# Moving the gates' softmax, the turning of the chosen indices and the first one-hots from behind run U into its last units

## The chip, the cores and the metric

The kernel runs on one core of a Trainium2 chip, in one launch. The metric is device time in microseconds (us). A core has five engines that run their own instruction streams and meet at semaphores: PE (TensorE, matmuls; PEld are its weight loads), ACT (ScalarE), DVE (VectorE), POOL (GpSimd) and SP (SyncE, which here issues the weights' DMAs). SBUF is the on-chip memory, PSUM the memory that matmuls write to.

## The reference

Two transformer blocks on 256 tokens of width 1024, in float32. Each block ends with a PEER layer: a mixture of 16,384 tiny experts of which each token picks 16 for each of 8 heads. Cut to what matters here:

```python
s_top, i_top = lax.top_k(s, 16)                  # on both halves of a query: 128 keys each
cand = s_top[..., 0, :, None] + s_top[..., 1, None, :]
best, ci = lax.top_k(cand.reshape(..., 256), 16)
i1, i2 = i_top[0][ci // 16], i_top[1][ci % 16]
e    = i1 * 128 + i2                             # which expert
gate = softmax(best, axis=-1)
act  = gelu(einsum("thkd,td->thk", u[e], x))
out  = einsum("thk,thkd->td", gate * act, v[e])
```

## The kernel before

The kernel gathers nothing. It works through *all* experts densely, in four stages for each block (b = 1, 2):

1. **Run U** (`u1`, `u2`): 128 units. A unit is one 128x1024 piece of `u`, multiplied with all 256 tokens; GELU of the product goes to `dense` (in `big`).
2. **The gates and indices.** While U runs, DVE does the top-16 searches in pieces between its other work: 64 steps, the last after unit 115. They leave `chosen`: for each token and each of its 128 picks i1, i2 and the score, tokens on partitions. Behind U come: subtract the best score (DVE, L1531 and L1532), exp (ACT, L1097), sum, reciprocal and scale (DVE, L1535 to L1537), a copy of `iota` to PSUM (L1539), the turn of `chosen` into picks on partitions (PE, six transposes, L748) and its copy back as `chosenT` and `neg_gate` (DVE, L1542 and L1543). The semaphore `ch_t` (printed as chosen_copied) then says that the turned arrays are there.
3. **The gate map**: for every token a 128x128 matrix of gates, made as a matmul of two one-hot matrices: hot1 (a 1 at i1, scaled by the gate) and hot2 (a 1 at i2). Tokens go in 64 maps of 4 tokens, in 8 groups of 8 maps (j = 0 to 7). Each token needs one hot1 tile of 128x128. POOL makes them for 14 of a group's 32 tokens (`POOL_HOTS`: slots j = 1, 3, 5, 7; L463). DVE makes those of slots 0 and 4 four at a time (L1555) and ACT scales them (L1105). ACT makes the other 10 with Abs and Relu (L1118, L1125). DVE makes all hot2, 8 tokens at a time (L1551, helper `hots`), and multiplies each pair of finished maps into `dense` (L1563, helper `apply`). PE makes a map of 4 tokens (L766), which the profile records as 8 matmuls.
4. **Run V** (`v1`, `v2`): 128 units of `v` against `dense`.

In U and V each weight tile is split into a high and a low float32r half: ACT makes `hi` (L984), DVE makes `lo` = raw - hi (L1619 in U, L1322 elsewhere), and PE multiplies three times (L573 and L575 need `hi`, L578 needs `lo`). `hi` and `lo` have a ring of 4 slots, which is 2 units, so ACT makes unit u's halves when PE has finished unit u-2. ACT also takes each unit's product from PSUM with GELU (L1019).

Order: there is no scheduler. Each engine's stream is written out by hand. PE and ACT issue the first group of 4 units of U straight, and the other 31 in a hardware loop (`Fori`); DVE's stream for U is straight throughout. POOL's one-hots wait for `ch_t`, and from the second group on also for PE: slot j of group g overwrites slot j of group g-1, so it waits until that map has been made (`wmap`, printed as gate_map). hot2 lies in `act_hi` and `act_lo`, which U's matmuls read; so DVE waits for U's last output (`taken`, printed as outs_taken) before it makes any. hot1 lies in `scores`, which is free when the last search is done.

Of the kernel before, what the change touches and what calls it, by code (L numbers as in the profile page):

```python
# [26 lines left out]
ALU = mybir.AluOpType  # L27
# [3 lines left out]
P = 128  # L31
# [15 lines left out]
EXP_TANH = "exp_and_others"  # L47
MAPS = 8
DVE_HOTS = (0, 4)
POOL_HOTS = ((1, 4), (3, 3), (5, 4), (7, 3))  # L50
ACT_HOTS = ((2, range(4)), (3, range(3, 4)), (6, range(4)), (7, range(3, 4)))

# [109 lines left out]
def two_blocks_kernel(nc, xT_in, memT_in, cols_in, front1, front2, u1, v1, u2, v2, biasA_in, gatew_in, keys_in,  # L162
                      ada_in, c_in, out):
    with ExitStack() as ctx:
# [192 lines left out]
        def is_static(v):  # L357
            return isinstance(v, int)

        def groups(eng, r, body, peel=1):  # L360

            n = r.units // GROUP
            for g in range(min(peel, n)):
                body(g)
            if n > peel:
                with eng.Fori(peel, n) as g:
                    body(g)


# [183 lines left out]
        def _(pe):  # L553
# [82 lines left out]
                    if after is not None:  # L636
                        after(u)

            def run(name, event=None, after=None, peel=None):

                r = RUNS[name]
                if event is not None:
                    pe.wait_ge(act_ready, 2 * EV[event] + 1)
                if r.kind != "O" and r.out0 and name not in CHAINED:
                    pe.wait_ge(taken, r.out0)

                def body(g):
                    for j in range(min(GROUP, r.units)):
                        for h in range(2):
                            if r.kind == "K":  # L650
                                outs_free(r, (g * GROUP + j) * 2 + (r.out0 + h))
                            elif h == 0 and r.kind != "O":
                                outs_free(r, g * GROUP + (r.out0 + j))
                            if event is not None and h == 1 and is_static(g) and j == 0:
                                pe.wait_ge(act_ready, 2 * EV[event] + 2)
                            half(r, g, j, h)
                        if after is not None and is_static(g):
                            after(g * GROUP + j)

                if r.units < GROUP:  # L660
                    body(0)
                else:
                    groups(pe, r, body, peel=peel or (1 if after is None else r.units // GROUP))

            def to_tokens(name):

# [76 lines left out]
            def gate_map(b):  # L743
# [5 lines left out]
                mm.then_inc(ch_tr, 1)  # L749

                def body(g):
                    for j in range(MAPS):
                        n = g * MAPS + (64 * (b - 1) + j)
                        if j in DVE_HOTS:
                            pe.wait_ge(hot_scaled, g * 2 + (16 * (b - 1) + DVE_HOTS.index(j) + 1))
                        for k, (slot, _) in enumerate(POOL_HOTS):
                            if slot == j:
                                pe.wait_ge(hot_pool, g * 4 + (32 * (b - 1) + k + 1))
                        for k, (slot, _) in enumerate(ACT_HOTS):
                            if slot == j:  # L760
                                pe.wait_ge(hot_act, g * 4 + (32 * (b - 1) + k + 1))
                        pe.wait_ge(hot2, g * 4 + (32 * (b - 1) + j // 2 + 1))
                        if not is_static(g) or g > 0 or b > 1 or j >= 4:
                            pe.wait_ge(w_done, g * 4 + (32 * (b - 1) + j // 2 - 1))
                        for t in range(4):
                            mm = pe.matmul(map_pairs[j // 2 % 2][:, j % 2, t * P:t * P + P], onehot[:, j, t, :],  # L766
                                           second_hot(j)[:, t, :].bitcast(F32), start=True, stop=True)
                        mm.then_inc(wmap, 1)

                body(0)  # L770
                with pe.Fori(1, 64 // MAPS) as g:
                    body(g)

            def experts(b):
                peer_scores(b, peer_q if b == 1 else peer_q2, keysA if b == 1 else keysB)
# [185 lines left out]
        def _(act):  # L961
# [24 lines left out]
            def run(name, evict=None, peel=1, after=None, lead=None, defer=False):  # L986

                r = RUNS[name]

                def body(g):  # L990
                    for j in range(min(GROUP, r.units)):
                        for h in range(2):
                            weight_hi(r, g, j, h)
                        if lead is not None and j == 0 and is_static(g) and g == 0:
                            lead()
                        if evict and not (j == 0 and is_static(g) and g == 0):
                            out(g * GROUP + (j - 1), (r.out0 + j - 1) % 2)
                        if after is not None:
                            after(g * GROUP + j)

                def out(u, b):
                    act.wait_ge(used, u * 2 + (r.half0 + 2))
                    evict(u, po[b]).then_inc(taken, 1)

                if r.units < GROUP:
                    body(0)
                else:
                    groups(act, r, body, peel=peel if after is None else r.units // GROUP)
# [78 lines left out]
            def experts(b):  # L1087
# [219 lines left out]
        def _(dve):  # L1307
# [202 lines left out]
            def experts(b):  # L1510
                r = RUNS[f"u{b}"]

                dve.wait_ge(sc_taken, 8 * b)
# [16 lines left out]
                g = chosen[:, 2, :, :].rearrange("p a (h k) -> p (a h) k", k=TOPK)  # L1530
                link(dve.tensor_copy(gsum[:, :], g[:, :, 0:1].rearrange("p a k -> p (a k)")))  # L1531
                dve.tensor_tensor(g, g, gsum[:, :].unsqueeze(2).broadcast_to([P, 16, TOPK]), ALU.subtract)\  # L1532
                    .then_inc(gate_sub, 1)
                dve.wait_ge(gate_exp, b)
                link(dve.tensor_reduce(gsum[:, :], g, AX.X, ALU.add))  # L1535
                link(dve.reciprocal(gsum[:, :], gsum[:, :]))
                dve.tensor_tensor(g, g, gsum[:, :].unsqueeze(2).broadcast_to([P, 16, TOPK]), ALU.mult)\  # L1537
                    .then_inc(gate_done, 1)
                dve.tensor_copy(iota_ps, iota[:, :])  # L1539
                dve.wait_ge(ch_tr, b)  # L1540
                for c in range(3):
                    dve.tensor_copy(chosenT[:, c, :], bx[c][:, 0:T])  # L1542
                link(dve.tensor_scalar(neg_gate[:, :], bx[2][:, 0:T], -1.0, None, ALU.mult))  # L1543
                dve.engine_nop().then_inc(ch_t, 1)  # L1544

                dve.wait_ge(taken, r.out0 + r.outs)

                def hots(g, pair):

                    key = chosenT[:, 1, bass.ds(g * 4 * MAPS + 8 * pair, 8)]  # L1550
                    dve.tensor_tensor(second_hot(2 * pair, 2), iota_ps.unsqueeze(1).broadcast_to([P, 8, P]),  # L1551
                                      key.unsqueeze(2).broadcast_to([P, 8, P]), ALU.is_equal).then_inc(hot2, 1)
                    if 2 * pair in DVE_HOTS:
                        key = chosenT[:, 0, bass.ds(g * 4 * MAPS + 8 * pair, 4)]
                        dve.tensor_tensor(onehot[:, 2 * pair, :, :], iota_ps.unsqueeze(1).broadcast_to([P, 4, P]),  # L1555
                                          key.unsqueeze(2).broadcast_to([P, 4, P]), ALU.is_equal)\
                            .then_inc(hot_dve, 1)

                def apply(g, pair):

# [386 lines left out]
```

## Time and profile before

| | |
|---|---|
| median of 3 runs | 2399.38 us (2398.82 to 2401.32) |
| profiled execution | 2402.24 us, of which its span is 2400.5 us |
| PE busy | 2277.1 us (95%) |
| DVE, ACT, POOL busy | 1681.8, 1264.8, 188.7 us |
| mean granted clock of PE | 0.983 of full speed |

The profile is of one execution. Its times count from the start of the span. In the first block U ends at about 748 us and the gate map's last product is applied at about 844 us; in the second block it is 1946 and 2041 us. A mean over the span says little about either: the stretch between U and V has its own limits, and is read by itself.

### The profile page before, as it was taken

To read this page: it belongs to the slowest core of one execution; us is meant where nothing else is said; L and a number is where in the kernel's file an instruction comes from. 1 tells how busy PE (TensorE), PEld (TensorE's weight loads), DVE (VectorE), ACT (ScalarE), POOL (GpSimd) and SP (SyncE) were. 2 spreads that over 40 slices of the span, in tenths; PEclk is the share of its full clock that TensorE was granted. 3 is DMA by queue.
4 is the path that set the end of the run, shared out by engine and by line. 5 is a ranking of instruction groups with operands and counts; after the bars stand their busy time and mean duration, and the time that the engine had idled before them with its cause. 6 is when DMAs were issued, how large, how long until landed. Compare 5 with 4: busy or idle time off the path is not lost.

```text
span 2400.5 us, 46390 instructions
## 1 busy us (share of the span) xinstructions
PE 2277.1 (95%) x15150; PEld 2075.6 (86%) x15150; DVE 1681.8 (70%) x3473; ACT 1264.8 (53%) x2761; POOL 188.7 (8%) x253
## 2 busy tenths in 40 slices
PE   5998899999998799999999999999999987999998
PEld 4996799999997688888888888999999976888887
DVE  7675665888886966666655557458888869666665
ACT  3453354555556855555556553445555568555554
POOL 0000000000004900000000000000000049000000
PEclk8998999999998999999999999999999999999999
DMA  9751254555552055555544334445555520555554
GB/s 372 286 195 36 84 213 142 183 182 181 181 184 87 0 189 192 194 193 193 176 141 145 111 106 154 141 144 184 181 183 179 183 79 0 182 194 192 192 192 149
DMA packets 106086, 389.82 MB, mean 162 GB/s; under 512 B 12032, under 2 KB 12160, under 8 KB 105232
## 3 DMA queue, kind: packets, MB, share of 16 engines
q1 hardware_dynamic: 104688, 381.73, 47.9%
q10 hardware_dynamic: 992, 4.88, 0.5%
q0 software_dynamic: 320, 2.13, 0.3%
q8 instruction: 46, 0.75, 0.1%
q14 instruction: 40, 0.33, 0.0%
HBM read 387.64 MB, written 1.05 MB: 162 GB/s over the span
## 4 chain that ended last, share of the span: by engine, by line
PE 83%; POOL 7%; DVE 5%; ACT 2%; DMA 1%; issue 1%; SPq 0%; POOLq 0%; DVEq 0%; ACTq 0%
PE ps L611 19%; PE ps L573 16%; PE ps L578 16%; PE ps L575 16%; PE ps L615 10%; POOL scores L463 7%; PE ps L634 1%; DMA big<-ada_in 1%; DVE lo L1322 1%; DVE act_lo L1399 1%; PE ps L739 1%; ACT big L1060 1%; PE ps L706 1%; DVE act_hi L1398 0%; DVE big L1426 0%
## 5 line engine op out<-in xcount | busy, mean ns | idle before, releaser
L984 ACT ACTIVATE hi<-raw 128x512 fp32r<-128x512 f32 x1340 | 768.6, 621 | 80.7 <-PE ps L578 78.4
L1322 DVE TENSOR_TENSOR lo<-raw,hi 128x512 fp32r<-128x512 f32 x828 | 536.9, 689 | 167.0 <-ACT hi L984 161.9
L573 PE MATMUL ps<-act_hi,hi 128*128 128x256 f32 x3312 | 541.6, 286 | 12.0 <-DVE act_lo L1399 5.5
L578 PE MATMUL ps<-act_hi,lo 128*128 128x256 f32 x3312 | 535.0, 284 | 6.8 <-DVE lo L1322 6.8
L575 PE MATMUL ps<-act_lo,hi 128*128 128x256 f32 x3312 | 534.3, 284 | 0.0
L573 PEld LDWEIGHTS ps<-act_hi,hi 128*128 128x128 f32 x3312 | 459.3, 193 | 24.9 <-issue 13.8
L578 PEld LDWEIGHTS ps<-act_hi,lo 128*128 128x128 f32 x3312 | 459.0, 193 | 8.0 <-DVE lo L1322 8.0
L575 PEld LDWEIGHTS ps<-act_lo,hi 128*128 128x128 f32 x3312 | 458.9, 193 | 0.0
L1619 DVE TENSOR_TENSOR lo<-raw,hi 128x512 fp32r<-128x512 f32 x512 | 329.8, 688 | 131.4 <-ACT hi L984 124.0
L611 PE MATMUL ps<-hi,act_hi 128*128 128x512 f32 x1024 | 398.9, 390 | 0.0
L611 PE MATMUL ps<-hi,act_lo 128*128 128x512 f32 x1024 | 398.4, 389 | 0.0
L1019 ACT ACTIVATE big<-ps 128x256 f32 (+1 forms) x338 | 130.2, 385 | 497.1 <-PE ps L578 497.1
L615 PE MATMUL ps<-lo,act_hi 128*128 128x512 f32 x1024 | 315.3, 389 | 0.0
L1594 DVE TENSOR_TENSOR act_lo<-big,act_hi 128x256 fp32r<-128x256 f32 x256 | 108.9, 426 | 248.5 <-ACT act_hi L1158 248.3
L1158 ACT ACTIVATE act_hi<-big 128x256 fp32r (+1 forms) x256 | 107.3, 419 | 325.5 <-PE ps L615 314.2
L463 POOL TENSOR_SCALAR scores<-iota,chosen 128x128 f32<-128x128 f32 x224 | 174.0, 789 | 1026.9 <-DVEq L1544 1026.9
L615 PEld LDWEIGHTS ps<-lo,act_hi 128*128 128x128 f32 x1024 | 192.2, 188 | 40.0
L611 PEld LDWEIGHTS ps<-hi,act_lo 128*128 128x128 f32 x1024 | 192.2, 188 | 39.9
L611 PEld LDWEIGHTS ps<-hi,act_hi 128*128 128x128 f32 x1024 | 192.2, 188 | 39.9
L766 PE MATMUL ps<-act_hi,scores 128*128 128x128 f32 x512 | 71.9, 294 | 25.8 <-POOL scores L463 13.0
L766 PEld LDWEIGHTS ps<-act_hi,scores 128*128 128x128 f32 x512 | 64.8, 203 | 32.6 <-POOL scores L463 17.3
L1563 DVE TENSOR_TENSOR big<-ps,big 128x1024 f32 (+1 forms) x64 | 78.1, 1220 | 13.1 <-PE ps L766 12.8
(213 smaller groups left out, 1590.5 us busy)
## 6 DMA issues: line engine op xcount, KB each, us to landing
raw<-u SPq DMA_DIRECT2D x256, 512.0 KB, 3.9
raw<-v SPq DMA_DIRECT2D x256, 512.0 KB, 4.3
raw<-front SPq DMA_DIRECT2D x166, 512.0 KB, 3.6
big<-ada_in SPq DMA_DIRECT2D x48, 512.0 KB, 5.5
big<-biasA_in ACTq DMA_DIRECT2D x1, 2048.0 KB, 10.0
xT<-xT_in ACTq DMA_DIRECT2D x1, 1024.0 KB, 10.2
big<-keys_in ACTq DMA_DIRECT2D x1, 1024.0 KB, 13.3
scores<-memT_in POOLq DMA_DIRECT2D x1, 1024.0 KB, 5.4
```

The source lines that it names most:

```text
L463: ins = pool.tensor_scalar(onehot[:, j, t, :], iota[:, :], chosenT[:, 0, tok:tok + 1], chosenT[:, 2, tok:tok + 1], ALU.is_equal, ALU.mult)
L573: pe.matmul(out_ap, hi_l(k), hi_r(k), start=(first and k == 0), stop=False, skip_group_check=True)
L575: pe.matmul(out_ap, hi_l(k), lo_r(k), start=False, stop=False, skip_group_check=True)
L578: mm = pe.matmul(out_ap, lo_l(k), hi_r(k), start=False, stop=(last and k == n - 1), skip_group_check=True)
L611: pe.matmul(vsum[tt][h], a[:, b, tt * P:tt * P + P], w_hi, start=False, stop=False, skip_group_check=True)
L615: mm = pe.matmul(vsum[tt][h], act_hi[:, b, tt * P:tt * P + P], w_lo, start=False, stop=False, skip_group_check=True)
L766: mm = pe.matmul(map_pairs[j // 2 % 2][:, j % 2, t * P:t * P + P], onehot[:, j, t, :], second_hot(j)[:, t, :].bitcast(F32), start=True, st ...
L984: act.activation(hi[:, s, :, :], raw[:, rs, 4 * h:4 * h + 4, :], ACT.Copy).then_inc(hi_done, 1)
L1019: return lambda u, p: act.activation(dst[:, bass.ds(u, 1), :].rearrange("p a t -> p (a t)"), p, func)
L1322: dve.tensor_tensor(lo[:, s, :, :], raw[:, rs, 4 * h:4 * h + 4, :], hi[:, s, :, :].bitcast(F32), ALU.subtract).then_inc(lo_done, 1)
L1594: dve.tensor_tensor(act_lo[:, j % 2, :], dense[:, bass.ds(u, 1), :].rearrange("p a t -> p (a t)"), act_hi[:, j % 2, :].bitcast(F32), ALU.s ...
L1619: dve.tensor_tensor(lo[:, s, :, :], raw[:, rs, 4 * h:4 * h + 4, :], hi[:, s, :, :].bitcast(F32), ALU.subtract).then_inc(lo_done, 1)
```

## The change

Line numbers of the changed program differ: before's L463 is L467 there, L573, L575, L578 are L577, L579, L582, L748 is L752, L766 is L772, L984 is L996, L1019 is L1031, L1097 is L1112, L1531 to L1543 are L1556 to L1570, L1551 is L1580, L1555 is L1535, L1563 is L1589, L1619 is L1645.

In both blocks the work of stage 2 is put at fixed units of U: the subtraction behind unit 117 on DVE, exp behind 118 on ACT, sum, scale and the copy of iota behind 120 on DVE, the six transposes behind 121 on PE, the copies and `ch_t` behind 123 on DVE. The two DVE hot1 instructions of group 0 (slots 0 and 4) stand behind units 124 and 125. For this PE and ACT leave their loop 3 groups earlier, and the last 12 units are issued straight.

```diff
+GATE_SUB_AT, GATE_EXP_AT, GATE_SUM_AT, GATE_TURN_AT, GATE_COPY_AT = 117, 118, 120, 121, 123
+GATE_TAIL = 3
@@ groups (all engines)
-                with eng.Fori(peel, n) as g:
+                with eng.Fori(peel, n - tail) as g:
+                    body(g)
+                for g in range(n - tail, n):
                     body(g)
@@ PE, experts
-                run(f"u{b}")
+                def after_expert(u):
+                    if u == GATE_TURN_AT:
+                        turn_chosen(b)
+                run(f"u{b}", after=after_expert, peel=1, tail=GATE_TAIL)
                 gate_map(b)
@@ ACT, experts
-                run(f"u{b}", to(dense, ACT.Gelu_apprx_tanh if b == 1 else ACT.Gelu))
-                act.wait_ge(gate_sub, b)
-                g = chosen[:, 2, :, :].rearrange("p a b -> p (a b)")
-                act.activation(g, g, ACT.Exp).then_inc(gate_exp, 1)
+                def after_expert(u):
+                    if u == GATE_EXP_AT:
+                        act.wait_ge(gate_sub, b)
+                        best = chosen[:, 2, :, :].rearrange("p a b -> p (a b)")
+                        act.activation(best, best, ACT.Exp).then_inc(gate_exp, 1)
+                run(f"u{b}", to(dense, ...), after=after_expert, tail=GATE_TAIL)
                 act.wait_ge(ch_t, b)
@@ DVE, experts, inside the loop over U's units
+                    if u == GATE_SUB_AT:
...
+                    if u == GATE_SUM_AT:
+                        dve.wait_ge(gate_exp, b)
...
+                    if u == GATE_COPY_AT:
+                        dve.wait_ge(ch_tr, b)
...
+                        dve.engine_nop().then_inc(ch_t, 1)
+                    if u in (GATE_COPY_AT + 1, GATE_COPY_AT + 2):
+                        first_hots(0, 2 * (u - GATE_COPY_AT - 1))
@@ DVE, hots
-                    if 2 * pair in DVE_HOTS:
+                    if 2 * pair in DVE_HOTS and not (is_static(g) and g == 0):
```

On ACT, the end of U in block 1. Before, the loop's last unit and what follows (names in brackets are the semaphores waited for; ACT_TABLE_LOAD brings in a set of functions):

```order
L984 ACTIVATE hi<-raw 128x512 [waits halves_used]
L1002 REGISTER_ALU
L1019 ISA [waits halves_used]
L1019 ACTIVATE big<-ps 128x256
L366 REGISTER_ALU
L366 COMPARE_AND_BRANCH
L1019 ACTIVATE big<-ps 128x256 [waits halves_used]
L1097 ACT_TABLE_LOAD
L1097 ACTIVATE chosen<-chosen 128x256 [waits topgate_sub]
```

Changed, units 118 to 119:

```order
L996 ACTIVATE hi<-raw 128x512 [waits halves_used,raw_loaded2]
L996 ACTIVATE hi<-raw 128x512 [waits halves_used]
L1031 ACTIVATE big<-ps 128x256 [waits halves_used]
L1112 ACT_TABLE_LOAD
L1112 ACTIVATE chosen<-chosen 128x256 [waits topgate_sub]
L996 ACTIVATE hi<-raw 128x512 [waits halves_used,raw_loaded3]
L996 ACTIVATE hi<-raw 128x512 [waits halves_used]
L1031 ACT_TABLE_LOAD
L1031 ACTIVATE big<-ps 128x256 [waits halves_used]
```

Exp and its table load stand inside U, and a second table load, back to GELU's set, stands before the next output.

On DVE, the end of U and the start of the gate map in block 1. Before:

```order
L1619 TENSOR_TENSOR lo<-raw,hi 128x512 [waits hi_done] x23
L1531 COPY gsum<-chosen 128x16
L1532 TENSOR_TENSOR chosen<-chosen,gsum 128x256 [waits dve_chain]
L1535 TENSOR_REDUCE gsum<-chosen 128x16 [waits topgate_exp]
...
L1543 TENSOR_SCALAR neg_gate<-ps 128x256
L1544 ISA [waits dve_chain]
L1551 TENSOR_TENSOR act_hi<-ps,chosen 128x1024 [waits outs_taken]
L1555 TENSOR_TENSOR scores<-ps,chosen 128x512
L1551 TENSOR_TENSOR act_hi<-ps,chosen 128x1024
L1551 TENSOR_TENSOR act_lo<-ps,chosen 128x1024
```

Changed:

```order
L1645 TENSOR_TENSOR lo<-raw,hi 128x512 [waits hi_done] x6
L1569 COPY chosen<-ps 128x256 [waits chosen_transposed]
L1569 COPY chosen<-ps 128x256 x2
L1570 TENSOR_SCALAR neg_gate<-ps 128x256
L1571 ISA [waits dve_chain]
L1645 TENSOR_TENSOR lo<-raw,hi 128x512 [waits hi_done] x2
L1535 TENSOR_TENSOR scores<-ps,chosen 128x512
L1645 TENSOR_TENSOR lo<-raw,hi 128x512 [waits hi_done] x2
L1535 TENSOR_TENSOR scores<-ps,chosen 128x512
L1645 TENSOR_TENSOR lo<-raw,hi 128x512 [waits hi_done] x4
L1580 TENSOR_TENSOR act_hi<-ps,chosen 128x1024 [waits outs_taken]
L1580 TENSOR_TENSOR act_hi<-ps,chosen 128x1024
```

`ch_t` (the ISA at L1571) is now given with 8 `lo` halves, which are 4 units, still to come; the four hot2 of group 0 are all that DVE has left between U's last output and the first `apply`.

## Rows read from the trace of the kernel before

**Rows 1.** The page's chain that ended last, by engine, shares of the span.
```profile
PE 83%; POOL 7%; DVE 5%; ACT 2%; DMA 1%; issue 1%; SPq 0%; POOLq 0%; DVEq 0%; ACTq 0%
```
**Rows 2.** That chain in order of time, block 1 (start us, length us, what).
```profile
747.42 0.49 PE ps L578 x4
747.93 0.38 ACT big L1019
748.34 1.28 ACT L1097
749.63 0.42 ACT chosen L1097
...
751.30 1.55 PE ps L748 x6
752.88 1.09 DVE chosen L1542 x3
...
754.46 87.03 POOL scores L463 x112
```
**Rows 3.** The same chain, block 2.
```profile
1945.01 0.49 PE ps L578 x4
...
1952.06 0.80 POOL scores L463
```
**Rows 4.** Who PE and DVE waited for, 741 to 848 us (total us, times, longest).
```profile
PE ps L766 <- POOL scores L463: 12.9, 20, 1.1
...
DVE big L1563 <- PE ps L766: 6.4, 8, 1.9
```
**Rows 5.** Busy us by stretch: PE, PEld, DVE, ACT, POOL; then granted clock, DMA, GB/s.
```profile
380.00:748.00 368.00, 367.90 (x3061) 367.69 (x3060) 302.44 (x782) 183.54 (x380) 0.00 (x0) 1.00 0.57 183
842.00:1195.00 353.00, 352.84 (x1561) 292.05 (x1559) 225.28 (x397) 190.58 (x395) 0.75 (x1) 1.00 0.59 193
```
**Rows 6.** Timeline of U's last units (start, length, engine, line; idle before, releaser).
```profile
742.55 1.15 ACT L984 ACTIVATE hi<-raw 128x512 fp32r<-128x512 f32 x2
743.21 1.29 DVE L1619 TENSOR_TENSOR lo<-raw,hi 128x512 fp32r<-128x512 f32 x2 [1.59 <-ACT hi L984]
744.86 0.64 PE L573 MATMUL ps<-act_hi,hi 128*128 128x256 f32 x4
745.82 0.64 PE L578 MATMUL ps<-act_hi,lo 128*128 128x256 f32 x4
```
**Rows 7.** Timeline of the gate map's first two groups, block 1.
```profile
756.25 1.28 ACT L1105 ACTIVATE scores<-scores,chosen 128x128 f32<-128x128 f32 x4 [6.21 <-DVE scores L1555]
757.44 1.27 ACT L1118 ACTIVATE scores<-iota,chosen 128x128 f32<-128x128 f32 x4
758.61 1.64 ACT L1125 ACTIVATE scores<-scores,chosen,neg_gate 128x128 f32<-128x128 f32 x4
760.97 1.27 ACT L1105 ACTIVATE scores<-scores,chosen 128x128 f32<-128x128 f32 x4
761.52 1.23 DVE L1563 TENSOR_TENSOR big<-ps,big 128x1024 f32 x1 [1.38 <-PE ps L766]
766.67 1.22 DVE L1563 TENSOR_TENSOR big<-ps,big 128x1024 f32 x1
769.53 1.22 DVE L1563 TENSOR_TENSOR big<-ps,big 128x1024 f32 x1
770.89 2.02 PE L766 MATMUL ps<-act_hi,scores 128*128 128x128 f32 x16 [0.90 <-DVE big L1563]
771.79 1.22 DVE L1563 TENSOR_TENSOR big<-ps,big 128x1024 f32 x1
```
**Rows 8.** Busy us and granted clock (third last) behind U, block 1.
```profile
750.00:752.00 2.00, 0.70 (x4) 0.70 (x5) 1.30 (x4) 0.05 (x1) 0.00 (x0) 0.50 0.00 0
```
**Rows 9.** Instructions that touch `chosen`: ns min/median/max, first and last start.
```profile
L463 POOL TENSOR_SCALAR scores<-iota,chosen x224: 783/787/801, 754.5 to 2038.3; 128x128 f32<-128x128 f32 x112
```
**Rows 10.** What PE's L573 matmuls waited for over the span (total us, times).
```profile
  issue: 14.4, 36
```

More of the change, by code:

```diff
@@ L358, in is_static, with groups @@
             return isinstance(v, int)
-        def groups(eng, r, body, peel=1):
+        def groups(eng, r, body, peel=1, tail=0):
             n = r.units // GROUP
@@ L637, in mem_run, with run @@
                         after(u)
-            def run(name, event=None, after=None, peel=None):
+            def run(name, event=None, after=None, peel=None, tail=0):
                 r = RUNS[name]
@@ L662, in run @@
                 else:
-                    groups(pe, r, body, peel=peel or (1 if after is None else r.units // GROUP))
+                    groups(pe, r, body, peel=peel or (1 if after is None else r.units // GROUP), tail=tail)
             def to_tokens(name):
@@ L741, in peer_scores, with turn_chosen @@
                     mm.then_inc(sc_ps, 1)
-            def gate_map(b):
+            def turn_chosen(b):
                 pe.wait_ge(gate_done, b)
@@ L749, in gate_map @@
                 mm.then_inc(ch_tr, 1)
+            def gate_map(b):
                 def body(g):
@@ L984, in weight_hi, with run @@
                 act.activation(hi[:, s, :, :], raw[:, rs, 4 * h:4 * h + 4, :], ACT.Copy).then_inc(hi_done, 1)
-            def run(name, evict=None, peel=1, after=None, lead=None, defer=False):
+            def run(name, evict=None, peel=1, after=None, lead=None, defer=False, tail=0):
                 r = RUNS[name]
@@ L997, in body @@
                             out(g * GROUP + (j - 1), (r.out0 + j - 1) % 2)
-                        if after is not None:
+                        if after is not None and is_static(g):
                             after(g * GROUP + j)
@@ L1007, in run @@
                 else:
-                    groups(act, r, body, peel=peel if after is None else r.units // GROUP)
+                    groups(act, r, body, peel=peel if after is None or tail else r.units // GROUP, tail=tail)
                 def last_out():
@@ L1093, in experts @@
                 act.preload_act_table(ACT.Gelu_apprx_tanh if b == 1 else ACT.Gelu)
-                run(f"u{b}", to(dense, ACT.Gelu_apprx_tanh if b == 1 else ACT.Gelu))
-                act.wait_ge(gate_sub, b)
-                g = chosen[:, 2, :, :].rearrange("p a b -> p (a b)")
-                act.activation(g, g, ACT.Exp).then_inc(gate_exp, 1)
+                def after_expert(u):
[3 more added lines that the diff above has]
+                        act.activation(best, best, ACT.Exp).then_inc(gate_exp, 1)
+                run(f"u{b}", to(dense, ACT.Gelu_apprx_tanh if b == 1 else ACT.Gelu), after=after_expert, tail=GATE_TAIL)
                 act.wait_ge(ch_t, b)
@@ L1511, in experts, with first_hots @@
                 r = RUNS[f"u{b}"]
+                g = chosen[:, 2, :, :].rearrange("p a (h k) -> p (a h) k", k=TOPK)
+                def first_hots(g, pair):
+                    key = chosenT[:, 0, bass.ds(g * 4 * MAPS + 8 * pair, 4)]
+                    dve.tensor_tensor(onehot[:, 2 * pair, :, :], iota_ps.unsqueeze(1).broadcast_to([P, 4, P]),
+                                      key.unsqueeze(2).broadcast_to([P, 4, P]), ALU.is_equal)\
+                        .then_inc(hot_dve, 1)
                 dve.wait_ge(sc_taken, 8 * b)
@@ L1536, in experts @@
[L1536 to L1543, printed above, removed]
@@ L1544, in experts @@
-                dve.engine_nop().then_inc(ch_t, 1)
+                        assert step < 64 or u < GATE_SUB_AT
+                    if u == GATE_SUB_AT:
+                        link(dve.tensor_copy(gsum[:, :], g[:, :, 0:1].rearrange("p a k -> p (a k)")))
+                        dve.tensor_tensor(g, g, gsum[:, :].unsqueeze(2).broadcast_to([P, 16, TOPK]), ALU.subtract)\
+                            .then_inc(gate_sub, 1)
+                    if u == GATE_SUM_AT:
+                        dve.wait_ge(gate_exp, b)
+                        link(dve.tensor_reduce(gsum[:, :], g, AX.X, ALU.add))
+                        link(dve.reciprocal(gsum[:, :], gsum[:, :]))
+                        dve.tensor_tensor(g, g, gsum[:, :].unsqueeze(2).broadcast_to([P, 16, TOPK]), ALU.mult)\
+                            .then_inc(gate_done, 1)
+                        dve.tensor_copy(iota_ps, iota[:, :])
@@ new lines, in experts @@
+                    if u == GATE_COPY_AT:
+                        dve.wait_ge(ch_tr, b)
+                        for c in range(3):
+                            dve.tensor_copy(chosenT[:, c, :], bx[c][:, 0:T])
+                        link(dve.tensor_scalar(neg_gate[:, :], bx[2][:, 0:T], -1.0, None, ALU.mult))
+                        dve.engine_nop().then_inc(ch_t, 1)
+                    if u in (GATE_COPY_AT + 1, GATE_COPY_AT + 2):
+                        first_hots(0, 2 * (u - GATE_COPY_AT - 1))
@@ L1552, in hots @@
                                       key.unsqueeze(2).broadcast_to([P, 8, P]), ALU.is_equal).then_inc(hot2, 1)
-                    if 2 * pair in DVE_HOTS:
[L1554 to L1557, printed above, removed]
+                    if 2 * pair in DVE_HOTS and not (is_static(g) and g == 0):
+                        first_hots(g, pair)
                 def apply(g, pair):
```

6 lines of the change are left out of this document (removed).

## The prediction

> **What bounds the kernel now.** I read the chain of waits by engine first. It is 83% PE and 7% POOL [rows 1], although POOL is busy for only 8% of the span, so POOL's work sits where nothing covers it. The chain in order of time says where: behind U's last matmul (747.42 + 0.49 = 747.91 us) come an output, a table load, exp, sums, transposes and copies, and only then 112 POOL one-hots in a row, 754.46 to 841.49 us, 0.777 us each [rows 2]. The map of the last POOL tile follows. In block 2 the same start is 1952.06, and U ends at 1945.01 + 0.49 = 1945.50 [rows 3]. So the start of POOL comes 6.55 us behind U in both blocks, and the gate map lasts as long as POOL needs. That PE there waits for POOL, 20 times, says the same [rows 4]. In U and V it is different: PE is busy for 367.9 of 368 us, at full clock [rows 5]. A thing put into U costs nothing on ACT and DVE as long as it stays within their lead, but every PE instruction in U is paid in full.
>
> **What the change moves, and the sum for block 1.**
>
> *The transposes.* Six of them, 1.55 us [rows 2], now stand between PE's units 121 and 122. They were on the path and are still: U ends at 747.91 + 1.55 = 749.46.
>
> *The work between U and POOL.* The table load 1.28, exp 0.42, the DVE operations and the copies leave the path. On DVE they fall into gaps: a unit's two `lo` take 1.29 us and the gap before them is 1.59 [rows 6]. The copies take 1.09 us and what follows them up to POOL's start 0.49 [rows 2], 1.58 together. They fit into one gap, and the sums, which lie between the end of exp at 750.05 and the transposes at 751.30 [rows 2], into another. The subtractions lead PE by more than that anyway: the first is done at 743.21 + 0.65 = 743.9 and is wanted at 745.82 [rows 6], 1.9 us later.
>
> *Exp on ACT* is the tightest place. The first half of `hi` starts at 742.55 and takes about 0.6, so it is there at 743.17; PE starts that unit at 744.86 [rows 6]. The lead is 1.69 us. Load and exp put in front take 1.28 + 0.42 = 1.70. That is even. The load back to GELU, 1.28, comes one unit later: ACT starts `hi` 1.71 late at 744.26, ends it at 745.40, loads to 746.68, takes the output to 746.96 and has the next `hi` at 747.6, wanted at 744.86 + 2.88 = 747.74. I take 0.1 us per block; the bounds are 0 and both loads in full, 2.6.
>
> *POOL's group 0.* Unit 127 starts at 744.86, so unit 125 ends at 741.98, and `lo` of 127 is done at 743.21 + 1.29 = 744.50 [rows 6], 2.5 us behind that. In the same way `lo` of 123 is done 2.5 us behind unit 121; with 1.58 for the copies `ch_t` comes at 4.1. From there to the end of U it is 1.55 + 6 x 2.88 - 4.1 = 14.7 us (a unit is 24 matmuls, and 3061 took 367.9 us [rows 5]: 2.88). POOL's 14 tiles of group 0 take 14 x 0.777 = 10.9 us, so they lie wholly beside U, where POOL did nothing. Group 1 still waits for maps of group 0, and these wait for hot2, which waits for U's last output.
>
> *The start of group 1 on POOL* is therefore the new start of the bound chain. From U's end at 749.46: the last GELU output, 0.02 + 0.38 [rows 2], to 749.86. Then side by side DVE's first hot2 (1.22 long) and ACT's scaling of slot 0, 1.28 [rows 7]: 751.15. Then PE makes maps 0 and 1, 2.02 us for both at full clock (the row at 770.89) [rows 7]: 753.2. POOL then has 98 tiles left, 98 x 0.777 = 76.15 us: it ends at 829.35 instead of 841.49. Written as a difference: 10.9 (group 0) + 6.55 (old start) - 5.3 (new start, transposes included) = 12.1 us.
>
> *What is late next.* Group 0 is now paced by ACT, which needs four pieces of it: scaling, Abs, Relu, one more tile, from 756.25 to 760.97, which is 4.72 for half a group [rows 7]. Its slot 2 is ready at 749.86 + 1.19 + 1.17 + 1.64 = 753.9. DVE's four hot2 end at 754.4, the first product at 755.6 to 756.8 (the bounds are a loop entry of nothing and of about 1.2), and map 4 needs it. Map 5 is then made at about 758.9, while POOL would like to start its third slot of group 1 at 753.2 + 7 x 0.777 = 758.6. I take 0.3 us for this wait. Later groups gain on it: DVE needs 2 x (2.86 + 2.26) = 10.24 us per group (products start at 766.67, 769.53, 771.79 [rows 7]), ACT 9.44, PE about 8.2, POOL 14 x 0.777 = 10.88. So POOL stays the bound.
>
> *PE's clock.* In the old order it is at the lower level (1.2 GHz) by 750, 2 us behind the end of U [rows 8]. Maps 0 and 1 could start when slot 0 was scaled, at 756.25 + 1.28 = 757.53, and their product starts at 761.52 [rows 7]: 4.0 us instead of 2.02. In the new order PE stands idle for only 1.7 us and then works in pieces. No row of the trace has just that. If the clock falls at once, the start of POOL's group 1 is 2.0 us later; if it falls a little later, it is mostly under POOL; if it stays, nothing. I take 0.8 per block, nearer to the middle, and keep 0 and 2.0.
>
> *DVE beside POOL.* In the old order every POOL tile runs beside DVE operations of which one input at least is in PSUM, and takes 783 to 801 ns, always the same [rows 9]. Now 14 run beside 8 `lo` subtractions, which have both inputs in SBUF. No row shows that pair. If each `lo` waits for one POOL tile, a unit costs DVE 2 x (0.78 + 0.65) = 2.9 us, plus 0.6 for a first hot1 behind units 124 and 125. Against the period of 2.88 that is 1.3 us of lag over both, under the lead of 1.9. And POOL's tiles, held up in turn by 8 x 0.65 = 5.2, need 16.1 us; they have 14.7 until U ends, and some 3.8 more until group 1 may start. So I price it at 0. The Trainium skill, in "SBUF — State Buffer", section "Who interferes with whom", says that a VectorE instruction with two SBUF inputs and a GpSimd instruction that reads SBUF share a port which one of them holds for its whole instruction. By that rule the pair does take turns, as in this price; if POOL's back-to-back tiles kept DVE out until they were all done, it would be rival B.
>
> *The straight tail.* PE's 12 last units are issued outside the loop. The first units of V are straight in the same way and show PE busy for 352.84 of 353 us [rows 5]. Price 0.
>
> **Sum.** Per block 12.1 - 0.3 - 0.8 - 0.1 = 10.9 us. Block 2 has the same start behind U, the same POOL work, so two blocks give 21.8 us. The profiled execution took 2402.24 us, of which the span is 2400.5, so the changed kernel would take 2380.4 by it. That execution lies 2.9 us above the median of the runs; against the median, 2399.38 - 21.8 = **2377.6 us**.
>
> **Rivals.**
>
> *A, the forecast*: 2374 to 2380, by the bounds of clock and waits. 2 x 12.1 gives 2375.2; with the clock's 2.0 and a wait of 0.3 per block, 2379.8.
>
> *B, POOL keeps DVE out.* POOL's 14 tiles run back to back for 10.9 us. DVE has a gap of about 1.5 before its next `lo` is due, and a lead of 1.9; the rest, 7.5 us, is PE standing still in U. It leaves 10.9 - 7.5 = 3.4 us of gain per block: 2392.6. For it: POOL leaves no gap between tiles [rows 2]. Against it: each instruction would have to win again over one that waits.
>
> *C, another engine takes over in the map.* DVE starts at 749.86, makes four hot2 in 4.5, has 7 groups of 10.24 and four products of 1.13 and ends near 831, where POOL's path ends at 829.7 + 1.0 + 1.2 = 831.9, one map and one product behind its last tile. The margin is 1 us. If DVE keeps meeting unfinished maps as it does now, 6.4 us in 8 waits [rows 4] of which the first, 1.4, belongs to the clock, it ends near 836 and the gain is 7.9 per block: 2383.6. Against it: those maps waited for POOL in their turn [rows 4], and POOL is ahead now.
>
> *D, ACT's two table loads are not covered*: 2.6 us of PE's time per block, and up to 1.7 more if the stop lets the clock fall. Gain 8.3 or 6.6 per block: 2383 to 2386. Against it: the lead is even with the first load and 0.15 ahead at the second.
>
> *E, slower: PE's straight tail is fed too slowly.* 24 units of the two blocks now come from code that runs once. Elsewhere PE has small stops that nothing in the profile explains, 14.4 us in 36 pieces, 0.4 each [rows 10]. With one at each switch between `hi` and `lo` products and between halves, 3 per unit, that is 1.2 x 24 = 28.8 us: 2399.4 - 21.8 + 28.8 = 2406.4. It decides from 21.8 / 24 = 0.91 us per unit. Against it stands V's straight start at full pace.
>
> **Chances.** A 0.71, B 0.05, C 0.11, D 0.10, E 0.03. Changes under 0.2% (4.8 us) can't be told from none here. A, C and D and nearly all of B are faster by more; a share of B and E goes to no change and to slower. Faster 0.95, same 0.03, slower 0.02. The range holds A, C and part of D: 2374 to 2384.5. A alone is 2374 to 2380.
>
> **What would show it.** In the changed profile: 14 POOL tiles before U's last matmul, the next about 5.3 us behind the old place of U's end (6.55 before), then 98 at 0.777 us without a gap but for a short one in group 1; the transposes inside U, and U 1.55 us longer. PE's stretch in U with no wait but perhaps a tenth at unit 119. Subtractions beside POOL that are longer or later, by less than 0.8 us. A clock that stays or falls for a few us. The forecast is wrong if PE waits in the tail for `lo` (B) or `hi` (D) by over 1 us, if POOL waits repeatedly after group 1 (C), or if PE's units in the tail are longer without a wait (E).

## The result: 1.0% faster, and the profile after

The changed kernel took 2376.10 us (median of 4 runs, 2375.11 to 2377.57) against 2400.04 us before in the same group of runs: ratio 0.9899, 95% interval 0.9887 to 0.9912. That is 23.9 us less, where 21.8 less was forecast. The span of the profiled execution fell from 2400.5 to 2375.2 us.

The page's chain by engine has no POOL left, where it had 7% [rows 1]:

```profile
PE 84%; DVE 10%; issue 2%; ACT 2%; DMA 1%; DVEq 0%; SPq 0%; ACTq 0%
```

The chain in order of time, block 1, answers to [rows 2]:

```profile
721.90 0.48 PE ps L582 x4
722.38 0.65 PE ps L577 x4
...
731.19 0.66 PE ps L752 x6
...
748.64 0.49 PE ps L582 x4
749.15 0.39 ACT big L1031
...
827.18 3.81 PE ps L772 x32
830.99 3.48 PE ps L794 x16
834.48 0.93 PE ps L615 x4
```

U now ends at 749.13, and V starts at 834.48: 85.35 us between. Before it was 747.91 and 846.18 (the row behind the clearing matmuls of that chain), 98.27. In block 2 the two are again 85.35 and 98.27. So the stretch lost 12.92 us in each block. U itself grew by two things: the transposes, 0.66, and one slow step at unit 119, 0.65 instead of 0.48. That is 0.83, so 12.1 us net per block, 24.2 in all. Between V's start in block 1 and U's in block 2 the profiled execution is 1.6 us shorter, and in front of the first U 0.5 longer. The change touches neither; in the profiled execution before, the clock fell once more there, at 1518 us, which it did not do in the one after.

Who waited in block 1 from 749 us on, for PE, DVE and POOL, answers to [rows 4]:

```profile
PE ps L772 <- DVE big L1589: 13.0, 20, 0.9
...
DVE big L1589 <- PE ps L772: 1.6, 2, 1.0
...
POOL scores L467 <- PE ps L772: 4.4, 1, 4.4
```

PE waited for POOL 20 times before. It now waits 20 times for DVE, DVE waits for PE 1.6 us instead of 6.4, and POOL waits once. The timeline of POOL (start, length, tiles, idle before) shows both stretches:

```profile
734.94 13.74 POOL L467 TENSOR_SCALAR scores<-iota,chosen 128x128 f32<-128x128 f32 x14 [486.97 <-DVEq L1571]
753.07 75.82 POOL L467 TENSOR_SCALAR scores<-iota,chosen 128x128 f32<-128x128 f32 x98 [4.39 <-PE ps L772]
```

Group 0 is ready at 748.68, before U ends. The other 98 tiles follow without a pause and end at 828.89. But the stretch does not end with them. The last four maps start at 827.18, when DVE has applied the pair of maps whose PSUM they overwrite, and run on to 830.99. DVE's own last two products wait for them:

```profile
829.24 1.23 DVE L1589 TENSOR_TENSOR big<-ps,big 128x1024 f32<-128x1024 f32 x1 [1.04 <-PE ps L772]
...
831.03 1.23 DVE L1589 TENSOR_TENSOR big<-ps,big 128x1024 f32<-128x1024 f32 x1 [0.56 <-PE ps L772]
```

The two places inside U. ACT around exp, answers to [rows 6]:

```profile
719.54 0.38 ACT L1031 ACTIVATE big<-ps 128x256 f32<-128x256 f32 x1 [1.46 <-PE ps L582]
719.94 1.28 ACT L1112 ACT_TABLE_LOAD   x1
721.23 0.42 ACT L1112 ACTIVATE chosen<-chosen 128x256 f32<-128x256 f32 x1
721.56 1.14 ACT L996 ACTIVATE hi<-raw 128x512 fp32r<-128x512 f32 x2
722.71 1.28 ACT L1031 ACT_TABLE_LOAD   x1
724.01 0.38 ACT L1031 ACTIVATE big<-ps 128x256 f32<-128x256 f32 x1
```

`hi` starts at 721.56, its first half takes about 0.6 us, and PE wants it at about 722.2; that is the 0.17 us of PE's slow step at 722.38. The second load costs nothing. And DVE's `lo` pairs beside POOL:

```profile
735.69 1.29 DVE L1645 TENSOR_TENSOR lo<-raw,hi 128x512 fp32r<-128x512 f32 x2 [0.91 <-ACT hi L996]
738.57 1.34 DVE L1645 TENSOR_TENSOR lo<-raw,hi 128x512 fp32r<-128x512 f32 x2 [0.99 <-ACT hi L996]
741.45 1.39 DVE L1645 TENSOR_TENSOR lo<-raw,hi 128x512 fp32r<-128x512 f32 x2 [0.94 <-ACT hi L996]
744.33 1.44 DVE L1645 TENSOR_TENSOR lo<-raw,hi 128x512 fp32r<-128x512 f32 x2 [1.49 <-ACT hi L996]
```

They are up to 0.15 longer. POOL's tiles over the whole span (ns min/median/max; before: [rows 9]):

```profile
L467 POOL TENSOR_SCALAR scores<-iota,chosen x224: 782/791/1839, 734.9 to 2012.0; 128x128 f32<-128x128 f32 x112
```

The median is that of before, but the longest tile is 1839 ns instead of 801. The long ones all lie in group 0 beside `lo`: in block 1 the second tile takes 1.84 us and three others 1.39 each, one beside each `lo` pair, and the other 10 take 0.79 or 0.80.

PE is busy for all of 380 to 748 us (before: [rows 5]), and at 750 to 752 its clock (third number from the end) is at the full 2.4 GHz, where it was at 1.2 [rows 8]:

```profile
380.00:748.00 368.00, 368.00 (x3064) 367.89 (x3063) 306.67 (x793) 185.99 (x382) 13.06 (x14) 1.00 0.58 182
...
750.00:752.00 2.00, 1.06 (x9) 1.09 (x10) 2.00 (x3) 2.00 (x8) 0.00 (x0) 1.00 0.00 0
```

### The profile page after: what moved, and what is told of

The parts are those of the page before. It is cut to its first block, busy times and chain, and to the rows that moved or that the text cites. A ratio compares the mean times of both kernels' runs of the same rounds, so it can differ in the third digit from the quotient of the medians.

```text
span 2375.2 us, 46239 instructions
## 1 busy us (share of the span) xinstructions
PE 2266.5 (95%) x15150; PEld 2067.6 (87%) x15150; DVE 1679.3 (71%) x3473; ACT 1264.8 (53%) x2763; POOL 193.7 (8%) x253
## 3 DMA queue, kind: packets, MB, share of 16 engines
q0 software_dynamic: 320, 2.13, 0.3%
HBM read 387.64 MB, written 1.05 MB: 164 GB/s over the span
## 4 chain that ended last, share of the span: by engine, by line
PE 84%; DVE 10%; issue 2%; ACT 2%; DMA 1%; DVEq 0%; SPq 0%; ACTq 0%
PE ps L615 20%; PE ps L577 16%; PE ps L582 16%; PE ps L579 16%; PE ps L619 10%; DVE big L1589 2%; PE ps L638 1%; DMA big<-ada_in 1%; DVE lo L1339 1%; DVE act_hi L1580 1%; DVE act_lo L1580 1%; DVE scores L1535 1%; DVE act_lo L1416 1%; PE ps L743 1%; ACT big L1072 1%
## 5 line engine op out<-in xcount | busy, mean ns | idle before, releaser
L996 ACT ACTIVATE hi<-raw 128x512 fp32r<-128x512 f32 x1340 | 767.8, 620 | 81.2 <-PE ps L582 78.5
L577 PE MATMUL ps<-act_hi,hi 128*128 128x256 f32 x3312 | 541.3, 286 | 12.0 <-DVE act_lo L1416 5.5
L582 PE MATMUL ps<-act_hi,lo 128*128 128x256 f32 x3312 | 534.2, 284 | 6.9 <-DVE lo L1339 6.9
L579 PE MATMUL ps<-act_lo,hi 128*128 128x256 f32 x3312 | 533.9, 284 | 0.0
L577 PEld LDWEIGHTS ps<-act_hi,hi 128*128 128x128 f32 x3312 | 458.4, 192 | 25.4 <-issue 14.2
L582 PEld LDWEIGHTS ps<-act_hi,lo 128*128 128x128 f32 x3312 | 458.3, 193 | 8.1 <-DVE lo L1339 8.1
L579 PEld LDWEIGHTS ps<-act_lo,hi 128*128 128x128 f32 x3312 | 458.5, 193 | 0.0
L1645 DVE TENSOR_TENSOR lo<-raw,hi 128x512 fp32r<-128x512 f32 x512 | 330.2, 689 | 124.4 <-ACT hi L996 116.9
L1031 ACT ACTIVATE big<-ps 128x256 f32 (+1 forms) x338 | 129.6, 383 | 492.3 <-PE ps L582 492.2
L467 POOL TENSOR_SCALAR scores<-iota,chosen 128x128 f32<-128x128 f32 x224 | 179.1, 817 | 994.2 <-DVEq L1571 985.5
L772 PE MATMUL ps<-act_hi,scores 128*128 128x128 f32 x512 | 65.4, 281 | 18.7 <-DVE big L1589 12.0
L772 PEld LDWEIGHTS ps<-act_hi,scores 128*128 128x128 f32 x512 | 59.6, 191 | 24.5 <-DVE big L1589 11.7
L1589 DVE TENSOR_TENSOR big<-ps,big 128x1024 f32 (+1 forms) x64 | 77.4, 1211 | 3.2 <-PE ps L772 3.2
```

The source lines that it names most:

```text
L467: ins = pool.tensor_scalar(onehot[:, j, t, :], iota[:, :], chosenT[:, 0, tok:tok + 1], chosenT[:, 2, tok:tok + 1], ALU.is_equal, ALU.mult)
L577: pe.matmul(out_ap, hi_l(k), hi_r(k), start=(first and k == 0), stop=False, skip_group_check=True)
L579: pe.matmul(out_ap, hi_l(k), lo_r(k), start=False, stop=False, skip_group_check=True)
L582: mm = pe.matmul(out_ap, lo_l(k), hi_r(k), start=False, stop=(last and k == n - 1), skip_group_check=True)
L1031: return lambda u, p: act.activation(dst[:, bass.ds(u, 1), :].rearrange("p a t -> p (a t)"), p, func)
L1589: dve.tensor_tensor(d, map_pairs[pair % 2].rearrange("p b (t i) -> p i (b t)", t=4), d, ALU.mult).then_inc(w_done, 1)
```

## The experiments

The theory behind them: POOL's early group is worth about half of the gain, the rest is the work taken from behind U; and the map's pace has passed to DVE, with POOL about 1 us from taking it back. The rivals: POOL alone still sets the pace; or POOL's early group only moves its wait; or the clock is what counts.

A difference of a few us is near the spread of the medians, so each trace is also read for one number, the *stretch*: from the start of the row of U's last `lo` product (L578 before, L582 after) to the start of V's first matmul. For the kernel before it is 747.26 to 845.83 = 98.57 in block 1 and 98.56 in block 2, for the changed kernel 748.48 to 834.13 = 85.65 and 85.65.

| run | median us | ratio to before, 95% interval | stretch, blocks 1 and 2 |
|---|---|---|---|
| r1 changed again | 2377.83 | 0.9904, 0.9889 to 0.9919 | 85.65, 85.65 |
| r2 POOL after U | 2388.74 | 0.9948, 0.9935 to 0.9962 | 92.25, 92.26 |
| r3 first hot1 in the map | 2382.32 | 0.9919, 0.9905 to 0.9932 | 87.90, 87.73 |
| r4 earlier clearing | 2373.66 | 0.9886, 0.9871 to 0.9901 | 84.83, 84.83 |
| r5 before, straight tail | 2401.25 | 1.0003, 0.9994 to 1.0012 | 97.54, 98.22 |
| r6 before, PE kept busy | 2400.13 | 0.9999, 0.9990 to 1.0009 | 97.90, 97.91 |
| r7 13 POOL tiles | 2375.72 | 0.9899, 0.9883 to 0.9916 | 85.65, 85.65 |
| r8 small DVE hot1 | 2375.68 | 0.9901, 0.9885 to 0.9918 | 84.75, 86.23 |
| r9 both cuts | 2370.21 | 0.9880, 0.9864 to 0.9897 | 82.54, 82.53 |
| r10 earlier clearing again | 2374.42 | 0.9894, 0.9877 to 0.9910 | 84.83, 84.83 |
| r11 changed, third time | 2375.16 | 0.9897, 0.9880 to 0.9913 | 85.65, 86.19 |

r1 to r4 ran as one group, r5 and r6, r7 to r9, and r10 and r11 as the others.

**r1, the yardstick.** No edit.

> The changed kernel once more, as the yardstick of this group: 2376 us, 24 under the kernel before. In its trace the map's end should again be set by DVE, which runs without a pause from U's last output, with POOL's last tile about 1 us from deciding.

Measured: 2377.83 us, 23.7 under the kernel before, and the same stretch to the hundredth. The chain again runs over DVE into PE's last four maps.

**r2, POOL waits for the end of U.**

```diff
                 pool.wait_ge(ch_t, b)
+                pool.wait_ge(taken, RUNS[f"u{b}"].out0 + RUNS[f"u{b}"].outs)
```

> The changed kernel, but POOL waits for U's last output before group 0; all else stays in U. Theory 1 (POOL's early group is most of the gain): 112 tiles at 0.777 = 87.0 us from about 749.6, so POOL ends at 836.6 instead of 828.9, 7.7 later. If DVE's chain is what ends last by about 1 us, 6.8 per block comes through: 2376.1 + 13.6 = 2389.7, up to 2391.5. Theory 2 (the gain is the softmax chain off the path and the clock; POOL's early group only lets it wait for maps instead): at most 3 us per block, under 2382.

Measured: 10.9 us over r1, and the stretch 6.6 longer in each block, where theory 1 had 6.8. POOL's timeline and two of DVE's `lo` rows in U's tail:

```profile
749.37 86.65 POOL L468 TENSOR_SCALAR scores<-iota,chosen 128x128 f32<-128x128 f32 x112 [501.89 <-ACT big L1032]
...
738.22 1.29 DVE L1646 TENSOR_TENSOR lo<-raw,hi 128x512 fp32r<-128x512 f32 x2 [0.98 <-ACT hi L997]
741.10 1.29 DVE L1646 TENSOR_TENSOR lo<-raw,hi 128x512 fp32r<-128x512 f32 x2 [0.99 <-ACT hi L997]
```

POOL has the chain again (112 tiles, then V), so its early group is worth 6.6 of the 12.9 us; theory 2 is out. The other 6.3 are what this kernel keeps over the kernel before: POOL starts 0.6 us behind U instead of 6.55, and its 112 tiles take 86.65 us instead of 87.03. Why a tile takes 0.774 us in some executions and 0.777 in others stays open. The two `lo` rows settle the longer `lo` of the changed kernel: without POOL beside them they take 1.29 each time, so POOL was the cause.

**r3, the first two hot1 of DVE back in the map.**

```diff
-                    if u in (GATE_COPY_AT + 1, GATE_COPY_AT + 2):
-                        first_hots(0, 2 * (u - GATE_COPY_AT - 1))
...
-                    if 2 * pair in DVE_HOTS and not (is_static(g) and g == 0):
+                    if 2 * pair in DVE_HOTS:
```

> The changed kernel, but the two DVE hot1 instructions of group 0 go back into the map. They cost DVE 2 x 0.6 = 1.2 us per block. If DVE's chain sets the end: 2376.1 + 2.4 = 2378.5. If POOL's does: slot 0 is scaled 1.1 + 0.6 later, so maps 0 and 1 and the start of group 1 come some 1.5 later: 2379. If neither counts: 2376. The difference between the first two is read from the trace: whether DVE has pauses in the map.

Measured: 4.5 us over r1 and the stretch 2.2 longer, nearly twice what I had from the instructions. PE's and POOL's timeline and PE's window (granted clock third from the end) show why:

```profile
752.57 5.47 PE L772 MATMUL ps<-act_hi,scores 128*128 128x128 f32 x32 [3.70 <-ACT scores L1122]
...
755.83 9.31 POOL L467 TENSOR_SCALAR scores<-iota,chosen 128x128 f32<-128x128 f32 x12 [7.39 <-PE ps L772]
...
754.00:756.00 2.00, 2.00 (x12) 2.00 (x11) 1.24 (x2) 1.97 (x7) 0.17 (x1) 0.50 0.00 0
```

Slot 0 is scaled later, so PE stands idle for 3.70 us instead of 1.82, and the clock falls during the first maps. POOL's group 1 starts 3.26 us behind the start of map 0 instead of 2.13. So POOL waits 7.39 us instead of 4.39: of these 3.0 us, 1.9 are the longer idle time and 1.1 the slower maps. POOL had 0.9 us to spare before it would set the end, and 3.0 less 0.9 is about the 2.2 measured; its last tile now ends at 831.78, and the last map 1.2 us behind it. DVE's chain is 2.1 later too, so both end nearly together. The second of my three cases had the path, through slot 0 to POOL, but not the clock.

**r4 and r10, a kernel that beats both?** 6 of the 8 accumulators of V are cleared before they are needed, in PE's idle time.

```diff
+                pe.wait_ge(ch_t, b)
+                clear(0, 4)
                 def body(g):
...
                 body(0)
+                clear(4, 6)
...
-                pe.wait_ge(ch_t, b)
-                for d in range(KT):
-                    pe.matmul(acc[:, d, :], zero..., start=(d % 2 == 0), ...)
+                clear(6, 8)
```

> The changed kernel, but PE clears the accumulators of V for 6 of 8 tiles earlier: 4 between U and map 0, where PE stands idle for 1.8 us, 2 behind group 0. In the changed kernel the 16 clearing matmuls stand 3.5 us between the last map and V, and end 1 us behind what V's first act_lo allows. Theory 1 (the clearing ends last there): V starts about 0.9 us earlier per block, 2376.1 - 1.9 = 2374.2. Theory 2 (the early clearing holds up map 0 or group 1 by as much as it saves): no change or up to 1 us slower.

> The kernel with the earlier clearing once more, beside the changed kernel on the same chip. In the first trace V started 0.82 us earlier behind U in each block, 1.6 together, so its median should be 1.6 below the changed kernel's. The 4.2 us between the medians of the first group then came mostly from elsewhere; if it is 4 again, the clearing gains more than its trace shows.

The stretch is 0.82 shorter in all four blocks of the two traces, as forecast. PE at U's end, and at V's start:

```profile
747.33 1.90 PE L757 MATMUL ps<-zero 128*128 128x256 f32 x8
...
829.21 1.03 PE L757 MATMUL ps<-zero 128*128 128x256 f32 x4
...
831.69 0.47 PE L615 MATMUL ps<-hi,act_hi 128*128 128x512 f32 x1 [1.45 <-ACT hi L1002]
```

V now waits for ACT's first weight half. The medians are 4.2 and 0.7 us below the changed kernel's of the same group; their intervals overlap, so the times do not show how much it is. The trace gives 1.6. It is the fastest complete kernel of the study: clearly faster than the kernel before, and faster than the changed one by the trace.

**r5, straight tail alone**: the kernel before with `tail=3` for U on PE and ACT.

> The kernel before, with U's last 3 groups of units on PE and ACT issued straight, and nothing else changed. Theory: straight code costs nothing, 2400 us as the kernel before, and in the trace PE's units in the tail still take 2.88 us. Rival E of the prediction: 0.4 us or more per unit, over 9.6 us slower for 24 units.

1.0003, interval 0.9994 to 1.0012. PE is busy for 364.00 of 364 us. Rival E is out. (Its stretch is 1.0 shorter in block 1 by two accidents: the clock fell only behind the transposes, which took 0.88 us, and POOL's tiles took 86.66 us instead of 87.03. In block 2 only the second holds, 0.3. So in block 1 the clock was still full behind 3.4 us without a matmul.)

```profile
380.00:744.00 364.00, 364.00 (x3036) 364.00 (x3035) 302.45 (x782) 182.95 (x379) 0.00 (x0) 1.00 0.60 183
```

**r6, the clock alone**: the kernel before, PE kept busy.

```diff
+                for _ in range(6):
+                    pe.matmul(po[0]..., ones[:, :], iota...)
                 pe.wait_ge(gate_done, b)
...
                 mm.then_inc(ch_tr, 1)
+                for _ in range(8):
+                    pe.matmul(po[0]..., ones[:, :], iota...)
```

> The kernel before, but PE fills its idle time between U and the transposes, and between the transposes and map 0, with 6 and 8 matmuls whose results nobody reads. It prices the clock. Theory: with the clock at full level the six transposes take 0.66 us as in the changed kernel instead of 1.55, so POOL starts 0.9 earlier; slow maps of group 0 cost nothing, since POOL sets the pace: 2 x 0.9 = 1.8 us faster, 2398.2. Rival: the slow maps count too, 2.0 per block more: 2394. Other rival: the filling matmuls delay the transposes, and it is slower than before.

The times do not tell it from the kernel before. The trace does: the stretch is 0.66 shorter, the transposes take 0.87 instead of 1.54, maps 0 and 1 take 2.05 instead of 4.

```profile
750.55 0.87 PE L752 MATMUL ps<-ident,chosen 128*128 128x128 f32 x6 [0.81 <-DVE chosen L1544]
...
753.04 9.35 POOL L463 TENSOR_SCALAR scores<-iota,chosen 128x128 f32<-128x128 f32 x12 [506.20 <-DVEq L1551]
...
756.17 2.05 PE L773 MATMUL ps<-act_hi,scores 128*128 128x128 f32 x16 [1.28 <-ACT scores L1112]
```

So in the old order only the transposes' share of the clock counted, 0.7 us; the slow maps lay beside POOL. The clock as such is not where most of the gain came from.

**r7, r8, r9: who sets the map's pace now?** Each leaves out part of hot1 from group 1 on.

```diff
# r7 and r9, POOL
-                        for t in range(n):
+                        for t in range(n - 1 if g and j == 5 else n):
# r8 and r9, DVE, first_hots
+                    n = 4 if is_static(g) and g == 0 else 1
-                    dve.tensor_tensor(onehot[:, 2 * pair, :, :], ...)
+                    dve.tensor_tensor(onehot[:, 2 * pair, 0:n, :], ...)
```

> The changed kernel with POOL making one tile fewer in each group from group 1 on (left out, the old tile is used again): 13 instead of 14, POOL's work in the map falls by 7 x 0.777 = 5.4 us per block. Theory 1 (DVE's chain now ends last): at most the 1 us of waits for late maps at the very end goes, 2374 to 2376. Theory 2 (POOL still sets the pace, as forecast): 2376.1 - 10.9 = 2365.

> The changed kernel with DVE's hot1 instructions from group 1 on made for 1 token instead of 4 (the other three left out): about 0.4 us each, 14 of them, 5.6 us per block off DVE's chain. Theory 1 (DVE ends last, POOL 1 us behind): POOL takes over at once, gain about 1 us per block, 2374. Theory 2 (POOL alone sets the pace): no change, 2376. Theory 3 (DVE alone, POOL far behind): 2376.1 - 11.2 = 2365.

> The changed kernel with both cuts: 13 POOL tiles per group and DVE's small hot1. If DVE and POOL are level now, as theory 1 has it, only both together bring the gain: 5 to 5.5 us per block, 2365 to 2366, while each alone brings 1 or less. If one of them alone sets the pace, this is no faster than the one that cuts it.

r7: no change in the stretch at all. 5.4 us less work on POOL buys nothing; POOL catches up and from 791 us on waits a little in every group. The groups start 10.24 apart, which is DVE's pace:

```profile
791.01 10.07 POOL L467 TENSOR_SCALAR scores<-iota,chosen 128x128 f32<-128x128 f32 x13 [0.18 <-PE ps L772]
801.25 10.07 POOL L467 TENSOR_SCALAR scores<-iota,chosen 128x128 f32<-128x128 f32 x13 [0.17 <-PE ps L772]
```

r8: 0.90 shorter in block 1, and there the chain is POOL's again, as theory 1 has it. In block 2 it is 0.58 *longer*. PE's and POOL's timeline there:

```profile
1932.68 5.44 PE L772 MATMUL ps<-act_hi,scores 128*128 128x128 f32 x32 [1.78 <-ACT scores L1122]
...
1936.33 75.82 POOL L467 TENSOR_SCALAR scores<-iota,chosen 128x128 f32<-128x128 f32 x98 [5.87 <-PE ps L772]
```

The clock fell behind an idle time of only 1.78 us, and POOL waited 5.87 instead of 4.39 in block 1: 1.48 us, straight into the end, since POOL sets it in this kernel.

r9: the stretch is 3.1 shorter in both blocks, and the median 5.5 below r7's and r8's. One cut alone brings 0 (r7) or 0.9 (r8), both together 3.1, so DVE and POOL were nearly level, and theories 2 and 3 are out. But 3.1 is not the 5 to 5.5 expected. A third engine comes into play, as PE's waits in block 1 show:

```profile
PE ps L772 <- ACT scores L1142: 9.2, 14, 0.7
PE ps L772 <- DVE act_hi L1581: 2.5, 2, 1.8
```

The maps come 9.67 us per group there, and in block 1 the chain runs over ACT and PE from 797 us to the end of the map (in block 2 only from 1997 us). I had ACT at 9.44 per group, twice its first half. That ACT is the next limit is read from the traces; no run makes ACT's work smaller to test it.

**r11, the changed kernel a third time.**

> The changed kernel for the comparison with the earlier clearing: about 2376 to 2378.

2375.16 us. In its block 2 the clock fell as in r8, with POOL's wait at 5.83, yet the stretch is only 0.54 longer: 0.9 of POOL's 1.44 us of delay were covered, as DVE ends that much behind POOL's path. The same idle time of about 1.8 us left the clock at full level in all other blocks of this kernel. POOL's timeline and PE's windows of block 2:

```profile
1934.84 75.81 POOL L467 TENSOR_SCALAR scores<-iota,chosen 128x128 f32<-128x128 f32 x98 [5.83 <-PE ps L772]
...
1930.00:1932.00 2.00, 0.77 (x5) 0.80 (x6) 2.00 (x2) 2.00 (x8) 0.00 (x0) 0.87 0.00 0
1932.00:1934.00 2.00, 2.00 (x11) 2.00 (x11) 2.00 (x3) 2.00 (x6) 0.00 (x0) 0.50 0.00 0
```

## Why the prediction was right, step by step

The mechanism was right in its main part: the work behind U is gone from the path, and POOL's group 0 lies beside U. The sum came 2.1 us short, by terms that partly cancelled. From U's end, POOL's last tile came 841.49 - 747.91 = 93.58 us later before and 828.89 - 749.13 = 79.76 later after: 13.82 less. From that tile to V it is 0.90 longer, since DVE ends behind POOL, and U is 0.83 longer: 12.1 per block, where 10.9 was forecast. The difference of 1.2 is, per block and rounded: +0.9 transposes, +0.8 clock, +0.3 the wait in group 1, +0.3 the 98 tiles (75.82 us instead of 76.15), -0.9 DVE's end, -0.2 the start of group 1, -0.1 exp. That the total came so near is in part luck: the bound that was missed took back 0.9 of the 2.3 us by which four other terms were too dear.

- *The transposes* were the term mis-sized most: 1.55 us by the row, 0.66 in U. The row was from a stretch at 1.2 GHz, which I had in my own rows [rows 8] and did not use. r6, at full clock in the old place, has 0.87, so 0.7 of the 0.9 us per block are the clock. The other 0.2 come with the place in a busy stretch; no run takes them apart.
- *Exp on ACT*: 0.1 forecast, 0.17 in the trace. "Even" was right: the first load shows, the second does not. D is out.
- *DVE's gaps* took the sums and copies without any wait of PE.
- *DVE beside POOL*: priced at 0, and 0 it is. POOL's 14 tiles take 13.74 us instead of 10.9, and `lo` pairs grow from 1.29 to up to 1.44 [rows 6, 9]. The delay is not spread evenly. Four of the 14 tiles carry it, by 0.6 us each or 1.05 in one case, about the time of one `lo` or two; no `lo` was held up by more than 0.15, though a tile takes 0.77. So nearly all of the waiting is POOL's. Both engines stay inside their leads. r2 shows that POOL is what lengthens `lo`. The Trainium skill, "SBUF — State Buffer", section "Who interferes with whom", has this pair as one that contends, and the trace agrees, with those numbers. B, which had DVE kept out for 10.9 us, is out. I had POOL at 16.1 us; it lost about half of what I allowed.
- *The start of group 1 on POOL*: 5.3 us behind U's old end forecast. Measured is 3.94 behind the new end plus 0.83, 4.77. So it came 0.53 earlier: 0.89 less for the transposes, 0.17 more for exp, and 0.19 more from U's end to POOL's start (3.94, forecast 3.75). The wait of 0.3 in group 1 did not come.
- *The clock*: 0.8 per block forecast. In the profiled execution it did not fall. In r8 and r11 it fell in one block of two and cost 1.48 and 1.44 at POOL's start. So the lower end, nothing, was met in most blocks, the upper end of 2.0 in none, and 0.8 was the cost of no block.
- *POOL stays the bound*: this step failed. I compared only the pace per group, 10.24 on DVE and 10.88 on POOL, and found 1 us of margin in the totals under rival C. DVE starts its chain 3.5 us before POOL's group 1, at 749.57, and is busy for 72.0 of the 72 us from 752 to 824. Up to its last four products my sum for it was right. These were put at 4 x 1.13 = 4.5 us, but take from 825.83 to 832.26, 6.4: PE can start the last four maps only at 827.18, when DVE has applied the first of the four products; they take 3.81, and DVE waits 1.04 and 0.56 for them. That loop of DVE to PE and back at the end was in no sum. C's mechanism came true without its price: DVE's waits shrank from 6.4 to 1.6 us, as I had argued against it, and those 1.6 were enough. It took 0.9 us per block off what POOL's path alone would have given (r8, block 1: that much came back).
- *E*: out by r5.

## What to carry to other kernels

When work is moved forward to shorten one engine's chain, add up every other engine's chain over the whole stretch, from its own new start to its own last instruction, with what its last steps wait for. The pace per step does not tell who ends last. Where engines are nearly level, a cut on one buys nothing (r7) or little (0.9 us in r8, block 1), and a cut on two buys 3.1 us (r9), less than the work taken out. Before a PE duration from a waiting stretch goes into a sum for a busy one, look at the granted clock of its row. And an idle time of PE behind which the clock falls in some executions, as the 1.8 us here, is a risk. Useful work can fill it, as the clearing matmuls of r4 do: the clock stayed full in all four gate maps of r4 and r10. As it did so in most maps without them too, these runs do not show that the filling is what kept it.

## What the runs showed of the hardware

- The same kernel with the same 1.8 us idle time of PE kept the clock at full level in five of its six gate maps and lost it in one (r11, block 2); r8 lost it in one of two; with 3.7 us (r3) it fell in both blocks. With 3.4 us it had fallen before the next matmul in the kernel before (transposes 1.54 us), but not in block 1 of r5 (0.88). Two instructions of 0.6 us on another engine cost 2.2 us in r3, of which the clock is about 1.1.
- POOL's and DVE's contention on SBUF is mild in this pairing: in a block, 8 subtractions grew by 0.15 us at most and kept their median of 0.69. Of 14 POOL tiles 10 kept their 0.79 us, three took 1.39 and one 1.84.
- A function table's load on ACT, 1.28 us, can be hidden in a stretch where ACT leads PE by 1.7 us. The first of two loads, with exp behind it, cost PE 0.17 us, and the second nothing.
